# Second block's mixer as one program per engine, with the attentions dealt among the gate units

## The reference

```python
aq, ak, av, bq, bk, bv, bf, cq, ck, cv, dq, dk, dv, diq, dik, diw = split(h @ w_in)
ya = diff_attention(rope(aq), rope(ak), av, lam)           # 4 pairs of heads: p0 - lam * p1, then a norm and a gain
yb = forgetting_attention(bq, bk, bv, bf + b_fgt)          # 4 heads, logits + cum[q] - cum[k] of log sigmoids
yc = stick_breaking_attention(cq, ck, cv)                  # 4 heads, strictly causal, no softmax
yd = indexed_sparse_attention(rope(dq), rope(dk), dv, rope(diq), rope(dik), diw, 64)
g = sigmoid(h @ w_gate + b_gate).reshape(B, S, 4, D)
merged = g[0] * (ya @ w_br_a) + g[1] * (yb @ w_br_b) + g[2] * (yc @ w_br_c) + g[3] * (yd @ w_br_d)
return merged @ w_out
```

## Time and profile before

| | us |
|---|---|
| median of 3 runs (lowest to highest) | 3954.48 (3952.47 to 3955.64) |
| the profiled execution | 3957.33 |
| its span, first to last instruction | 3955.2 |
| PE busy | 3521.4 (89%) |
| DVE busy | 2074.1 (52%) |
| ACT busy | 1405.8 (36%) |
| POOL busy | 249.0 (6%) |
| mean granted PE clock, of full speed | 0.933 |

### The profile page before, as it was taken

How to read it: one execution, slowest core, us unless ns; L and a number is a source line. 1 busy time by engine, 2 the same in 40 slices (tenths; PEclk the granted TensorE clock), 3 DMA queues, 4 the chain that set the end, 5 groups by cost and what they waited for, 6 DMA issues and landing times. The chain is left out here.

```text
span 3955.2 us, 54418 instructions
## 1 busy us (share of the span) xinstructions
PE 3521.4 (89%) x20670; PEld 3010.3 (76%) x20670; DVE 2074.1 (52%) x2729; ACT 1405.8 (36%) x2278; POOL 249.0 (6%) x169
## 2 busy tenths in 40 slices
PE   5999897789998999898899999769899999769899
PEld 4888642467887888764799999548899999548898
DVE  5767474547677433214465555554455555554454
ACT  3323302333333322212444444243344444243443
POOL 1000100100001000200001011200001011200000
PEclk8999997889999999998899999879999999879999
DMA  6666420026665233420166664104466665104464
GB/s 203 182 180 175 115 72 22 0 59 169 183 175 161 82 100 91 101 96 1 43 177 175 173 179 146 52 1 121 132 180 172 174 178 154 44 0 127 133 180 133
DMA packets 766419, 478.37 MB, mean 121 GB/s; under 512 B 35093, under 2 KB 743173, under 8 KB 766101
## 3 DMA queue, kind: packets, MB, share of 16 engines
q1 hardware_dynamic: 755872, 473.14, 42.2%
q10 hardware_dynamic: 10356, 2.63, 0.4%
HBM read 474.65 MB, written 1.05 MB: 120 GB/s over the span
## 5 line engine op out<-in xcount | busy, mean ns | idle before, releaser
L535 PE MATMUL psum<-normed,weights_part 128*128 128x256 f32 (+1 forms) x11232 | 1744.2, 317 | 50.5 <-DVE weights_part L521 18.1
L535 PEld LDWEIGHTS psum<-normed,weights_part 128*128 128x128 f32 x11232 | 1593.0, 193 | 185.5 <-issue 35.1
L521 DVE TENSOR_TENSOR weights_part<-weights,weights_part 128x2048 fp32r<-128x2048 f32 (+1 forms) x397 | 848.5, 2140 | 774.6 <-ACT weights_part L513 774.6
L513 ACT ACTIVATE weights_part<-weights 128x2048 fp32r<-128x2048 f32 (+1 forms) x397 | 708.0, 1786 | 789.7 <-PE psum L535 373.1
L535 PE MATMUL psum<-hidden,weights_part 128*128 128x256 f32 (+1 forms) x4224 | 681.0, 323 | 1.6 <-DVE hidden L1116 1.6
L535 PEld LDWEIGHTS psum<-hidden,weights_part 128*128 128x128 f32 x4224 | 614.5, 190 | 63.4 <-DVE hidden L1116 2.0
L1300 DVE SCALAR_TENSOR_TENSOR stage<-weights,cond,stage 128x768 f32<-128x768 f32 x294 | 281.0, 1018 | 0.0
L408 POOL TENSOR_TENSOR square<-square,rinvs 128x256 f32<-128x256 f32 (+1 forms) x39 | 65.1, 1670 | 2470.3 <-ACT rinvs L393 2468.7
L1020 ACT ACTIVATE rinvs<-psum 128x256 f32<-128x256 f32 (+1 forms) x88 | 39.7, 451 | 216.8 <-PE psum L535 216.8
L887 DVE TENSOR_REDUCE negmax<-psum 128x1 f32<-128x256 f32 (+1 forms) x128 | 66.8, 523 | 94.7 <-PE psum L2389 19.7
L1131 DVE SCALAR_TENSOR_TENSOR x<-psum,gate,x 128x256 f32<-128x256 f32 (+1 forms) x112 | 49.5, 478 | 119.9 <-PE psum L535 119.9
(11 more groups left out here) (303 smaller groups left out, 3252.2 us busy)
## 6 DMA issues: line engine op xcount, KB each, us to landing
weights<-in_l_ffn_w_in SPq DMA_DIRECT2D x176, 512.0 KB, 5.2
weights<-in_ffn_w_gu SPq DMA_DIRECT2D x176, 512.0 KB, 5.0
weights<-in_l_mod_w SPq DMA_DIRECT2D x168, 384.0 KB, 3.4
weights<-in_w_in SPq DMA_DIRECT2D x34, 1024.0 KB, 5.2
weights<-in_w_gate SPq DMA_DIRECT2D x64, 512.0 KB, 4.6
weights<-in_l_ffn_w_out SPq DMA_DIRECT2D x64, 384.0 KB, 4.2
weights<-in_ffn_w_down SPq DMA_DIRECT2D x64, 384.0 KB, 4.0
weights<-in_l_ffn_w_out SPq DMA_DIRECT2D x64, 320.0 KB, 3.4
```

The source lines that it names most:

```text
L513: k.nc.scalar.activation(k.parts[part][0][:, W], k.slots[slot][:, W], ACT.Copy).then_inc(k.high_done, 1)
L521: k.nc.vector.tensor_tensor(k.parts[part][1][:, W], k.slots[slot][:, W], k.parts[part][0][:, W].bitcast(F32), ALU.subtract).then_inc(k.spl ...
L535: mm = k.nc.tensor.matmul(to, left[a], right[b], start=first and n == 0, stop=last and n == len(PASSES) - 1)
```

## The change

The eight blocks of a mixer become one, in which each engine runs a single program: `project`, `gates_and_attention`, `merge_branches`.

- The norm runs chunk by chunk under the first unit of the projection. The heads a to d, the index heads and keys are kept two to a tile (queries of two heads in rows 0 to 63 and 64 to 127, keys of each with zeros in the other half); heads are rotated right after their unit: one turn of 512 columns on PE, a product on POOL, a product and a sum on DVE. The index unit moves to place 4 and has 24 passes. POOL zeroes whole key tiles at the start, SP waits for two of these memsets and loads the selector ahead of the weights.
- The gate units (`gates_b`, 16) are separate from the branches (`branch_b`, 8). The gates stay closed (bias added, no sigmoid) in tiles that are free by then.
- The attentions are cut into steps. Two steps go with a gate unit: one after the first tile of 24 passes, one after the second. The logits of the eight pairs are formed at steps 1, 4, 7, 10, 13, 16, 21, 24. Only causal blocks are formed: 128 queries with 128 keys, and 128 with 256, two heads at a time. The diagonal's mask is one fp32r pass. There is no staging of queries. The norm of the a heads works on rows, before they are turned.
- The branches run by themselves after the gates, as plain float32 products, and the merged chunks are split as they come; the output product's first unit follows chunk by chunk.
- The tables of sines and cosines are made for rows 64 to 79 too; the constants are smaller by 384 columns.

The diff, cut to its core (the old functions `project_heads`, `log_sigmoids`, `score_keys`, `take_best`, `mask_others`, `stick_breaking`, `second_attentions` and the loop of `merge_branches` are removed):

```diff
+        add(f"gates_b{l}", N_GATES, opened, 2, looped=False)
+        add(f"branch_b{l}", KD, branches, 4, looped=False, parts=0)
...
+PROJECTED = (("aq", 0), ("aq", 1), ("iq", 0), ("iq", 1), ("index", 0), ("ak", 0), ("ak", 1), ("bq", 0), ("bk", 0), ("dq", 0),
+             ("dk", 0), ("va", 0), ("va", 1), ("cq", 0), ("ck", 0), ("bv", 0), ("cv", 0), ("dv", 0))
...
+    @block.gpsimd
+    def _(pool):
+        for name in ("bq", "bk", "ak", "ik", "dk", "ck"):
+            nc.gpsimd.memset(k.head[name], 0.0).then_inc(t["zeroed"].sem, 1)
+        for c in rotated:
...
+                last = nc.gpsimd.tensor_tensor(in_pairs(by_cos(c)), in_pairs(raw(c)), both(k.cos2), ALU.mult)
...
+                    if tt == 0 and c - 1 in order:
+                        turn(c - 1)
...
+ATTENDED = ("a", "a", "a", "a", "b", "b", "d", "d")
+LOGITS_AT = (1, 4, 7, 10, 13, 16, 21, 24)
+KEY_SCORES_AT = (3, 6, 9, 12)
+STICKS_AT = (2, 10)
+ROOT_AT, TURN_A_AT = 15, 17
+BEST_AT = range(13, 21)
...
+        for s in range(N_GATES):
+            gate_tile(s, 0)
+            if s == 0:
+                pe.wait_ge(k.banks_free, RING + first)
+            step(2 * s)
+            gate_tile(s, 1).then_inc(k.unit_done, 1)
+            step(2 * s + 1)
+
+    @block.scalar
+    def _(act):
+        def exponents(j):
+            if j >= 2:
+                act.wait_ge(t["probs_turned"].sem, t["probs_turned"].base + 2 * (j - 1))
+            act.wait_ge(t["maxed"].sem, t["maxed"].base + 2 * j + 2)
+            for qt in range(2):
+                for hh in range(2):
+                    at = 2 * qt + hh
+                    nc.scalar.activation(prob[j % 2][:, hh, queries[qt]], S[:, hh, queries[qt]], ACT.Exp,
+                                         bias=k.negmax2[:, j % 2, at:at + 1],
+                                         accum_out=k.rowsum2[:, j % 2, at:at + 1]).then_inc(t["exped"].sem, 1)
...
+        def step(n):
+            if n in LOGITS_AT:
+                exponents(LOGITS_AT.index(n))
+            if n in KEY_SCORES_AT:
+                rectify(KEY_SCORES_AT.index(n))
+            for j, at in enumerate(LOGITS_AT):
+                if n == at + 3:
+                    copy_odd(j)
+                if n == at + 5 and j < A:
+                    square_rows(j)
...
+        for s in range(N_GATES):
+            step(2 * s)
+            wait_product(k, act, spec, 0, s)
+            if s + 2 < N_GATES:
+                split_high(k, act, 0, first + s + 2)
+            step(2 * s + 1)
+            open_gates(s)
...
+        for s in range(N_GATES):
+            if s >= 1 and s + 1 < N_GATES:
+                split_low(k, dve, 0, first + s + 1)
+            step(2 * s)
+            step(2 * s + 1)
...
+            if c >= KD - 2:
+                split_high(k, act, 0, out.start + c - KD + 2)
+            high(c)
...
+            zeroed, landed = k.tally("in_zeroed"), k.tally("in_selector_landed")
+            sp.wait_ge(zeroed.sem, zeroed.base + 2)
+            sp.dma_start(k.head["bk"][HD:HD + 4, :, :], k.selector).then_inc(landed.sem, 16)
+            sp.dma_start(k.head["bq"][HD + 32:HD + 36, :, :], k.selector).then_inc(landed.sem, 16)
+            load_weights(k, sp, first.start + RING, min(out.start + out.n + RING, total))
```

More of the change, by code:

```diff
@@ L273, in weight_plan, with opened, branches @@
         ffn("ffn1", f"_b{l}", w["ffn1_w_gu_2"][l], w["ffn1_w_down_2"][l], 4)
[L275 to L278, removed]
+        listed(f"in_b{l}", w["w_in_2"][l], projected_units(whole), 2)
         gates = w["w_gate_2"][l].rearrange("(k p) (b n) -> p b k n", p=P, b=4)
         br = {n: by_chunk(w[f"w_br_{n}_2"][l]) for n in "abcd"}
[L282 to L292, removed]
+        def opened(slot, i, c, gates=gates):
+            return [(pair_tiles(slot)[:, t], gates[:, gate, :, c // 2 * P:(c // 2 + 1) * P]) for t, gate in enumerate(GATES_OF[c % 2])]
+        def branches(slot, i, c, br=br):
+            return [(tall_tile(slot)[:, row:row + rows, :], br[name][:, :, c * P:(c + 1) * P])
+                    for name, row, rows in (("a", 0, 4), ("d", 4, 2), ("b", 6, 2), ("c", 8, 2))]
+        add(f"gates_b{l}", N_GATES, opened, 2, looped=False)
+        add(f"branch_b{l}", KD, branches, 4, looped=False, parts=0)
         wide(f"out_b{l}", w["w_out_2"][l], 4)
@@ L1958, in project_heads @@
[L1958 to L1993, removed]
-                else:
[L1996 to L2046, removed]
@@ new lines, in project @@
+    names = ("scaled", "copied", "normed", "zeroed", "raw", "turned", "by_cos", "by_sin", "rotated", "forget", "forget_ready",
+             "log_sigmoid", "summed_forget", "dots", "lambda_exp", "lambda_sum", "selector_landed")
+    t = {n: k.tally("in_" + n) for n in names}
+    rotated = [c for c, (name, _) in enumerate(PROJECTED) if name in ROTATED]
+    order = {c: r for r, c in enumerate(rotated)}
+    index = [name for name, _ in PROJECTED].index("index")
+    rows = [k.roots[:, 1, T], k.rinvs[:, 1, T]]
@@ new lines, in project, with bank, turn_bank, raw @@
+    forget, low, cum, ones_row = (k.gate_rows[0:4, n, T] for n in range(4))
+    K = slice(HD, P)
+    def bank(c):
+        return k.psum[:, 2 * ((first + c) % RING)]
+    def turn_bank(c):
+        return k.psum[:, 2 * ((first + c) % RING) + 1]
+    def raw(c):
+        return k.square[:, order[c] % 2, :]
+    def by_cos(c):
+        return k.roots[:, order[c] % 2, :]
+    def by_sin(c):
+        return k.rinvs[:, order[c] % 2, :]
+    def both(table):
+        return table.unsqueeze(1).broadcast_to([P, 2, LAT])
```

1038 lines of the change are left out of this document (696 added, 342 removed).

## The result

The changed kernel takes 3632.18 us (median of 4 runs, 3628.36 to 3638.19), beside 3955.06 for the kernel before (4 runs): ratio 0.918, 95% interval 0.916 to 0.920. The forecast was 3646, in a range from 3614 to 3727. The profiled execution took 3628.36 (span 3626.6), 329.0 less than that of before.

The account below looks back on a forecast made before the run. PE was taken to bound the dense stages and latency the attentions. Per mixer 113.3 + 150 + 35.3 + 25 = 323.6 us, from 478.0; 308.8 saved in both layers gave 3646, range 3614 to 3727.

Parts of the forecast that it names:

- the 0 of the bounds 0 and 5.6: Projection: Pool's zeroing of key tiles beside the norm was taken to cost 0 us, with bounds 0 and 5.6.
- Gates with attention: Stage of gate units with attention steps dealt among them: 150 us a mixer, bounds 136.5 and 185.
- Sum 14: Gates stage: exposed PE waits, 10 us behind the odd-probability copy plus 3.8 for table loads, on top of 136.5.
- The floor, 136.5: Gates stage: PE's own work, 92.2 us for the gates and 44.3 for the attentions, all waits hidden.
- 4.6 us against 2.9: Gates stage: from logits' end through reductions, exponents and odd copy 4.6 us, against a 2.9 us tile of 24 passes.
- Six times: Gates stage: six times a pair's weighting waits 1.7 us for ACT's odd copy behind the next pair's exponents, 10 us.
- The three table loads, 3.8: Gates stage: three pairs (1, 4, 5) find another function's table on ACT, 1.28 us each, 3.8 together.
- Projection: Norm and projection of one mixer: 113.3 us, with PE waiting 1.4 at the index unit.
- Branches and output: After the gates stage: branches with opening the last gate 35.3 us, output product 25 us.
- All hidden: Rival: the gates stage comes out at its floor and the tail at 24, total 3616; chance 0.12.
- ACT's order rules: Rival: splits and gate openings ahead in ACT's order add some 35 us, stage 185, total 3716; chance 0.22.
- Slower, the clock: Rival: new waits hold PE at 1.2 GHz through the mixer, 122 us a layer slower, total 4200; chance 0.03.

Follow-up runs that it names:

- f32_masks: The changed kernel with causal and strict masks added by f32 products, as in the kernel before, instead of one-pass products: 3643.0 us, ratio 0.921.
- norm_wait: The changed kernel with unit 0 of the projection waiting for all eight normed chunks instead of chunk by chunk: 3644.6 us, ratio 0.922.
- odd_first: The changed kernel with ACT copying a pair's odd probabilities ahead of the next pair's four exponents: 3624.0 us, ratio 0.916.
- coarse: The changed kernel with two attention steps after each whole gate unit (48 passes) instead of one after each tile of 24: 3684.9 us, ratio 0.932.
- coarse_odd: Two attention steps after each whole gate unit, and ACT's odd-probability copy ahead of the next exponents, against the changed kernel: 3649.9 us, ratio 0.923.
- sigmoid_early: The changed kernel with gates opened by the sigmoid in the attention stage, and the branches' pass of sigmoids left out: 3644.8 us, ratio 0.921.

## Why the prediction was right, and where it was off

The time lies in the range and 14 us under the forecast. Of the 8.9 us by which the sum for one mixer was too high, 8.8 are in the gates stage; the other terms are not off in ways that cancel. Of the six waits a layer that were to show the mechanism, three came, of 0.5 to 1.8 us.

**What bounds the kernel.** Latency in the attentions, PE in the dense stages: shown. Alone, the same attention instructions need 100.5 us; dealt among gates they add 45 + 4. `f32_masks` shows the other side: work given to PE now costs its length.

**Projection.** 113.0 against 113.3. Unit 0 ends 9.2 us after the norm begins (9.3), and one unit alone waits, 1.08 (1.4). Pool's six memsets lay beside the norm, and DVE's operations there kept their 0.42 to 0.48: the 0 of the bounds 0 and 5.6 was right. `norm_wait` prices the chunk-by-chunk start at 5.7 us a layer.

**Gates with attention.** The term that was mis-sized is "Sum 14", the exposed waits. The floor, 136.5, was 1 us short: with every wait away the stage's PE work is 137.5. On top came 3.7 a layer (`odd_first`, the branches' wait apart), not 14. Two errors made it. First, "4.6 us against 2.9" for the odd copy's chain: its own terms add up to 4.4, and it is 3.5, since I added accumulator reads and ACTIVATEs at full length though they overlap. Second, "Six times": behind the logits of pairs 2, 3 and 4 PE has 1.4 to 1.7 us of stick work in the same gap, so that the first two of these waits vanished and the third shrank to 0.2. I had counted that work in the floor and not as cover. The three table loads, 3.8, were exposed once, at the sqrt; the first lay in idle time of ACT, the second under the stick work but for those 0.2. The mechanism (the copy's place in ACT's order) was right and the only one.

**Kept gates.** The prediction gave them no price of their own. About 7 us a layer, 3.7 of it in waits.

**Branches and output.** 36.0 and 24.5 against 35.3 and 25. Chunk 7 is low 6.1 us after the branches end (6.5).

**Rivals.** All hidden gave 3616: the changed kernel lies between it and my 3646, and with its waits removed it stands at 3624. ACT's order rules (185 us of stage): in the changed kernel no split or opening stands ahead of any wait in the stage. With the coarse tables a split does, but it costs under 1 us in `coarse` and some 2 us in `coarse_odd`, not 35. Slower, the clock: its condition did not arise, but the mechanism is real. Every wait of 2.8 to 4.6 us in the coarse tables was followed by PE at 1.2 GHz; in `coarse` that cost 9 us on 16.8 of waits, half as much again. The prediction read the Trainium skill (TensorE: Matmul & The Clock Gate, Part 1) so that waits of 1 to 3 us would leave the clock alone; the rows below don't always agree. The 2.66 us a switch that the Trainium skill gives (ScalarE: Activation LUTs, What ACT_TABLE_LOAD costs) is not borne out: 1.28 in every row shown, and ACT's busy time grew by some 20 us for 15 more loads.

## What to carry to other kernels

Deal latency-bound steps among dense work so that each hand-over has a dense piece of its own length in it, and count the other small jobs in the same gap as cover before you price a wait. What an in-order engine does for the waiting one goes ahead of what has slack: here one moved copy was worth 6 us in a fine table and 35 in a coarse one. Price a chain by the distance between starts, not by sums of durations, and a long wait at its own length plus the slow clock behind it. Before you credit an edit with 1 us, look at the stretches that it left alone: here one unit swung by 1.4.

## What the runs showed of the hardware that I had not expected

One wait, in the same place and of the same length (1.76 to 1.77 us, PE busy before and behind), appears in ten mixers of five profiled kernels: the changed one, the same again, `f32_masks`, `sigmoid_early` and `norm_wait`. In six of them the next tile starts 2.16 us after the weighting begins; in four it starts 3.2 to 3.9 us after, and that tile is slow as well. The changed kernel's four mixers are all among the six. What decides it no run here shows. The Trainium skill (TensorE: Matmul & The Clock Gate, Part 1) says that the same kernel can meet the change of level at a different point in another run. The changed kernel's two runs show no such difference, but the two mixers of one run do, in `sigmoid_early` and in `norm_wait`. Length alone doesn't settle it either: a wait of 1.77 us at pair 6 in `sigmoid_early` and one of 1.81 in `coarse` were followed by full pace in both mixers. Two outcomes for one wait are another reason to remove it: in `odd_first` no wait is left between the gate tiles.

After a wait the clock need not be low at once: in `coarse`, behind a wait of 3.71 us, PE ran at full pace for about 1 us and then at half.

```profile
3267.72 0.39 PE L2349 MATMUL psum<-attended,weights 128*128 128x128 f32 x2
3267.94 0.40 PE L2347 MATMUL psum<-attended,weights 128*128 128x128 f32 x2
3268.16 0.61 PE L2348 MATMUL psum<-attended,weights 128*128 128x128 f32 x2
3268.57 0.64 PE L2349 MATMUL psum<-attended,weights 128*128 128x128 f32 x2
```
